# Low parts of the weights in a buffer of their own, with rows 64 bytes off the 512-byte grid

## The reference

```python
h = x + (o * silu(r)) @ gla_w_out          # q, k, v, r, g_low = rms_norm(x) @ gla_w_in
h = h + relu(rms_norm(h) @ mlp_w_up) ** 2 @ mlp_w_down
x = rms_norm(h)
p = rms_norm(x) @ w_in_2                   # q, k, v, three branches, three gates
x = x + (g_a * (attn @ w_attn_o_2) + g_b * (lru @ w_lru_o_2) + g_c * (conv @ w_sc_o_2)) @ w_out_2
x = x + relu(rms_norm(x) @ w_mlp_up_2) ** 2 @ w_mlp_down_2
out = rms_norm(x)
```

## Time and profile before

| | |
|---|---|
| median of 3 runs | 2735.91 us (2735.05 to 2736.26) |
| profiled execution | 2733.07 us, its span 2731.0 us |
| mean granted TensorE clock | 0.996 |
| TensorE busy | 2706.4 us, 99% |
| weight loads busy | 2368.7 us, 87% (beside the matmuls) |
| VectorE busy | 1796.6 us, 66% |
| ScalarE busy | 1348.8 us, 49% |
| DMA | 504 MB, mean 185 GB/s |

### The profile page before, as it was taken

The page is one execution under the profiler, slowest core; times in us unless marked ns, Lnnn a source line. Parts: engine busy times, 40 slices in busy tenths (PEclk is TensorE's granted clock), DMA queues, the critical chain, the costliest instruction groups (busy, mean ns, idle before and its releaser), DMA issues.

```text
span 2731.0 us, 43584 instructions
## 1 busy us (share of the span) xinstructions
PE 2706.4 (99%) x15627; PEld 2368.7 (87%) x15627; DVE 1796.6 (66%) x2074; ACT 1348.8 (49%) x1628; POOL 86.8 (3%) x69
## 2 busy tenths in 40 slices
PE   8999999999999999999999999999999999999998
PEld 7888888888888888888888888888888888888887
DVE  6666867656566567766887666666676566565664
ACT  4546555444444445544575554555554444444443
POOL 3000010000000001200000000000100000000000
PEclk9999999999999999999999999999999999999999
DMA  6564666666566665575546565555656566665653
GB/s 184 161 205 127 185 191 189 191 191 184 192 187 193 189 189 188 181 220 174 173 155 196 188 192 188 190 185 192 191 187 191 185 188 194 187 191 189 189 185 131
DMA packets 507074, 504.45 MB, mean 185 GB/s; under 512 B 17731, under 2 KB 505432, under 8 KB 506984
## 3 DMA queue, kind: packets, MB, share of 16 engines
q1 hardware_dynamic: 505820, 501.60, 59.1%
q10 hardware_dynamic: 1164, 1.63, 0.2%
HBM read 499.50 MB, written 3.67 MB: 184 GB/s over the span
## 4 chain that ended last, share of the span: by engine, by line
PE 98%; DVE 1%; issue 0%; ACT 0%; POOL 0%; DVEq 0%; POOLq 0%; ACTq 0%
PE acc L478 60%; PE acc L480 31%; PE acc L473 3%; PE acc L475 2%; PE misc L578 0%; PE misc L593 0%; PE misc L697 0%; PE misc L535 0%; DVE wsp L1017 0%; PE misc L494 0%; POOL ssq L434 0%; PE misc L560 0%; PE misc L541 0%; PE misc L646 0%; PE misc L595 0%
## 5 line engine op out<-in xcount | busy, mean ns | idle before, releaser
L1017 DVE TENSOR_TENSOR wsp<-raw,wsp 128x1024 fp32r<-128x1024 f32 x944 | 1167.5, 1244 | 597.9 <-ACT wsp L751 567.8
L478 PE MATMUL acc<-xs,wsp 128*128 128x512 f32 x4224 | 1478.9, 395 | 7.8 <-DVE wsp L1017 7.8
L751 ACT ACTIVATE wsp<-raw 128x1024 fp32r<-128x1024 f32 x944 | 992.6, 1056 | 712.2 <-PE acc L480 649.1
L480 PE MATMUL acc<-xs,wsp 128*128 128x256 f32 x4224 | 1180.7, 280 | 0.0
L478 PEld LDWEIGHTS acc<-xs,wsp 128*128 128x128 f32 x4224 | 792.9, 188 | 189.7 <-DVE wsp L1017 9.4
L478 PE MATMUL acc<-hs,wsp 128*128 128x512 f32 x2560 | 890.2, 393 | 0.0
L480 PEld LDWEIGHTS acc<-xs,wsp 128*128 128x128 f32 x4224 | 798.4, 189 | 0.4
L480 PE MATMUL acc<-hs,wsp 128*128 128x256 f32 x2560 | 713.1, 279 | 0.0
L478 PEld LDWEIGHTS acc<-hs,wsp 128*128 128x128 f32 x2560 | 479.5, 187 | 108.7
L480 PEld LDWEIGHTS acc<-hs,wsp 128*128 128x128 f32 x2560 | 482.2, 188 | 0.0
L760 ACT ACTIVATE corr<-acc 128x512 f32<-128x512 f32 x248 | 148.4, 598 | 411.5 <-PE acc L480 392.3
(11 more groups left out here) (213 smaller groups left out, 1016.2 us busy)
## 6 DMA issues: line engine op xcount, KB each, us to landing
raw<-in_w_in SPq DMA_DIRECT2D x224, 512.0 KB, 4.2
raw<-in_mlp_w_up SPq DMA_DIRECT2D x128, 512.0 KB, 4.0
raw<-in_mlp_w_down SPq DMA_DIRECT2D x128, 512.0 KB, 4.1
raw<-in_w_mlp_up SPq DMA_DIRECT2D x128, 512.0 KB, 4.0
raw<-in_w_mlp_down SPq DMA_DIRECT2D x128, 512.0 KB, 4.2
raw<-in_gla_w_in SPq DMA_DIRECT2D x96, 512.0 KB, 3.8
raw<-in_gla_w_out SPq DMA_DIRECT2D x32, 512.0 KB, 4.4
raw<-in_w_out SPq DMA_DIRECT2D x32, 512.0 KB, 4.0
```

The lines of the kernel that those rows point to most:

```text
L478: pe.matmul(acc[:, g, j], wsp[:, slot, t, 0, cols], x[:, k0 + k], start=start, stop=False, skip_group_check=True)
L480: ins = pe.matmul(acc[:, g, j, 1], wsp[:, slot, t, 1, cols], x[:, k0 + k, 0], start=False, stop=stop, skip_group_check=True)
L751: act.activation(wsp[:, slot, :, 0], raw[:, slot], ACT.Copy).then_inc(hi_done, 1)
L1017: dve.tensor_tensor(wsp[:, slot, :, 1], raw[:, slot], wsp[:, slot, :, 0].bitcast(F32), ALU.subtract).then_inc(lo_done, 1)
```

## The change

`wsp` becomes one flat tensor: first the high parts of all slots and row groups, 16 KB, then a gap of 16 elements (64 bytes), then the low parts, 16 KB, and a rest that fills it up to 32 KB + 512 bytes. `w_part(k, slot)` is the high (k = 0) or low (k = 1) part of a slot, four row groups of 256 columns in one run. `both_parts(slot, t)` is one row group with both parts, 16,448 bytes apart. What follows in SBUF moves by 512 bytes. Matmuls, splits, semaphores and their order stay as they are.

```diff
     raw = at("raw", [P, SLOTS, UK, NB])
-    wsp = at("wsp", [P, SLOTS, UK, 2, NB], F32R)
+    LOWS = SLOTS * UK * NB + 16
+    wsp = at("wsp", [P, 2 * SLOTS * UK * NB + P], F32R)
+
+    def w_part(k, slot):
+
+        n = UK * NB
+        return wsp[:, k * LOWS + slot * n:k * LOWS + (slot + 1) * n].rearrange("p (t n) -> p t n", t=UK)
+
+    def both_parts(slot, t):
+
+        row = (slot * UK + t) * NB
+        return wsp[:, 0:2 * LOWS].rearrange("p (k n) -> p k n", k=2)[:, :, row:row + NB]
+
@@ gemm
                         if tokens_out:
-                            pe.matmul(acc[:, g, j], x[:, k0 + k, 0, cols], wsp[:, slot, t], start=start,
+                            pe.matmul(acc[:, g, j], x[:, k0 + k, 0, cols], both_parts(slot, t), start=start,
                                       stop=False, skip_group_check=True)
-                            ins = pe.matmul(acc[:, g, j, 1], x[:, k0 + k, 1, cols], wsp[:, slot, t, 0],
+                            ins = pe.matmul(acc[:, g, j, 1], x[:, k0 + k, 1, cols], w_part(0, slot)[:, t],
                                             start=False, stop=stop, skip_group_check=True)
                         else:
-                            pe.matmul(acc[:, g, j], wsp[:, slot, t, 0, cols], x[:, k0 + k], start=start,
+                            pe.matmul(acc[:, g, j], w_part(0, slot)[:, t, cols], x[:, k0 + k], start=start,
                                       stop=False, skip_group_check=True)
-                            ins = pe.matmul(acc[:, g, j, 1], wsp[:, slot, t, 1, cols], x[:, k0 + k, 0],
+                            ins = pe.matmul(acc[:, g, j, 1], w_part(1, slot)[:, t, cols], x[:, k0 + k, 0],
                                             start=False, stop=stop, skip_group_check=True)
@@ split_hi
-            act.activation(wsp[:, slot, :, 0], raw[:, slot], ACT.Copy).then_inc(hi_done, 1)
+            act.activation(w_part(0, slot), raw[:, slot], ACT.Copy).then_inc(hi_done, 1)
@@ split_lo
-            dve.tensor_tensor(wsp[:, slot, :, 1], raw[:, slot], wsp[:, slot, :, 0].bitcast(F32),
+            dve.tensor_tensor(w_part(1, slot), raw[:, slot], w_part(0, slot).bitcast(F32),
                               ALU.subtract).then_inc(lo_done, 1)
```

## The result

The changed kernel takes 2731.42 us (median of 20 runs, 2730.31 to 2733.04), the kernel before 2737.15 in the 20 runs beside it. The ratio is 0.995, with a 95% interval of 0.9929 to 0.997: a small gain, far from the 4% of the forecast.

What follows compares the result with a forecast made beforehand. TensorE's matmul spacing was taken to bound the kernel. From the profiled 2733.1 us, -98 for low-part loads, -4 for the slower pattern and +2 for waits gave 2633.1; 2.8 more for the median made 2636 us, range 2590 to 2745.

Steps and rivals of the forecast that it cites:

- What the excess is: In the weight stream, each pair of matmuls takes 26.7 ns more than its columns need, 201 us in all.
- The first two readings: In the weight stream: the excess isn't other engines' traffic; a weight load starts with each matmul, reading SBUF beside x.
- The third: The excess is no fixed instruction price: the same instructions also run at 353.8 ns a pair, so two streams stall each other.
- The bound of -13 ns: Long matmul beside the low part's load: its gap falls from 230 to 217 ns, as with the plain fp32 matmuls.
- The term of -98 us: Loads of low parts, 64 bytes off the grid: 7552 pairs gain 13 ns each.
- the slower pattern goes with the change: In the weight stream, 22 of the 236 blocks lose their slower pattern, 0.19 us each: -4 us.
- The +2 us for TensorE's waits: At the hooks of attention and recurrence blocks, a faster TensorE waits more; 7.8 us could double at worst, taken as +2.
- The gv and v blocks: 384 pairs with weights as moving operand, read as two runs: cost 0 to 3 us, taken as 0.
- High parts taken at 0: Loads of high parts beside the short matmul: between 0 and -10 ns a pair, taken as 0.
- No change: Rival, 2736 us, chance 0.29: the full-rate read stalls by itself, or 64 bytes don't affect how the reads collide.
- Slower: Rival, 2785 us, chance 0.16: the long gap settles into the slower pattern, 7.1 ns a pair, +49 us.
- More gained: Rival, 2572 us, chance 0.05: the short gap falls too, a pair takes 326 ns, -160 us with other terms.

Runs made afterwards that it cites:

- the long execution: The kernel before, unchanged, run again until one of its slow executions was profiled: 2761.06 us.

## Why the prediction was wrong

**What bounds the kernel** was right: TensorE's spacing, and no wait near it. The waits for the splits went from 7.8 to 9.6 us and all other work kept its durations.

**What the excess is: the step that failed.** The first two readings hold. The third compared 346.7 with 353.8 ns at equal operands and took it for proof that the whole excess of 26.7 ns is a meeting of two reads, which an offset can end. It proves that for the 6.7 ns between the rhythms only. The runs divide the excess otherwise:

- 7.8 ns are there with a stream that doesn't walk (327.8 ns a pair).
- 18.9 ns need the stream's walk. Against them stand the 6.7 that went with the high parts at 192 bytes and the low parts at 0 (340.0 ns): a part of the excess can indeed be moved by the offset of the loads. If these 6.7 are a part of the 18.9, which no run shows by itself, 12.2 are left that stayed in all nine layouts.
- The offset of the change, low parts at 64 bytes, took nothing from the 346.7 ns. It only ended the 353.3 of the usual blocks.

A load without a walk took nothing away either (346.7), and one with a quarter of the columns 3.4 ns (343.3). So most of the 12.2 ns are probably the stream's own. That isn't shown, as no run has such a stream without a load beside it.

**The bound of -13 ns** rested on the earlier trace rows, where the load was the same and the read half as fast. The prediction read from it that the two reads don't disturb each other there. But the stream that needs new bytes with every column was absent too, and with every column read twice a pair takes 327.5 ns with its loads untouched. So the earlier trace rows can't tell a meeting from a stall of the stream alone, and its 217 ns were no price for an offset. The term of -98 us measured zero: 2886 matmuls beside 2887. The best layout has long gaps of 227 ns and short ones of 113, beside 230 and 117.

**The small terms.** That the slower pattern goes with the change, 22 blocks and -4 us, came true for the usual blocks (3.4 us beside the profiled execution) and is nearly the whole gain of a short execution: about 2736 to 2731 us. Its reason, that the pattern goes together with the excess, was not the right one, since the excess stayed. As a forecast of the median it was undersized, as the profile was of one of the best executions: 36 blocks are slow in another, and in the long ones more than a hundred, where the change gives back some 28 us. The prediction saw three runs within 1.2 us and had no sign of that. The +2 us for TensorE's waits measured +1.8, by luck: they were to come from a faster TensorE, and in its long stretches it wasn't faster. The gv and v blocks were bounded from 0 to 3 us and taken at 0. Beside the profiled execution they cost about 1 us. TensorE alone from 1230 to 1270 us, in the profiled execution of the kernel before, then in the changed kernel:

```profile
1230.00:1270.00 40.00, 40.00 (x232) 1.00 0.65 197
```

```profile
1230.00:1270.00 40.00, 40.00 (x229) 1.00 0.64 195
```

**High parts taken at 0** because neither operand changed its remainder: the number was right, the short gap is still 117 ns. The bound of the whole 10 ns was never reached: with the high parts at 192 bytes the short gap is 113.

**The rivals.** "No change" had the sizes nearly right, 3.3 ns for each matmul and a sixteenth of the stream: the stream without its walk leaves 7.8 ns a pair (5.7 and 2.1), and the walk's 18.9 are a seventeenth of the 320 ns of columns. That this stall comes "whatever is loaded beside it" holds for some 12.2 ns of it at most. Its time was off by the slow rhythm alone. "Slower" was priced for the change and came true for its neighbour: with both parts off by 64 bytes every pair takes 353.3 ns, 2778 us beside the 2785 foretold. "More gained" at 2572 us would have needed the part to go that hangs on the stream's walk: even without the walk the time was 2600.78.

The Trainium skill's two read ports ("TensorE: Matmul & The Clock Gate", step-by-step section) fit the larger part: a load with or without a walk leaves the pair at 346.7 ns. They don't fit the rest. With the same instructions and streams, the place of the loads alone moves a pair from 340.0 to 353.3 ns, and the measurement decides: a load isn't free for the matmul beside it.

**What stays open.** How the 12.2 ns divide between the stream and the mere presence of a load. Why an offset picks its rhythm: the table repeats after 256 bytes in the one case tried, and neither the distance of low to high parts nor that of a load to its stream orders it. Why a stretch falls into one rhythm or the other behind a hook isn't shown either; that it keeps it until the next break is.

## What to carry to other kernels

If a stream of matmuls runs with a constant excess, first read whether it comes in more than one rhythm: the distance between them is a part that can be moved. It is no bound, as 340.0 ns never came in the kernel before. It doesn't explain the rest either, which needs its own test, such as an operand that doesn't walk, before it is priced. A kernel whose times lie in two heaps may have both heaps in its own instruction spacing, so profile one execution of each heap before looking outside. Offsets of operands are cheap to try and not to be foretold: nine layouts of one buffer gave 2683 to 2779 us, and the one that was chosen here was not the best.

## What the runs showed of the hardware

- 18.9 ns of a pair (768 columns of fp32r, granted clock 1.00) hang on a moving operand with new bytes in every column: 346.7 ns with it, 327.8 with one column read again and again, 327.5 with every column read twice. Offsets of the loads alone brought 340.0; if those 6.7 ns are among the 18.9, at most 12.2 are the stream's own.
- Without the walk 5.7 and 2.1 ns are left above the columns: gaps of 219.0 and 108.8 ns for 213.3 and 106.7.
- The offset of the stationary operands, with the moving ones left in place, moves a pair among 340.0, 346.7, 350.0 and 353.3 ns, which are all multiples of 3.33 ns. Low parts at 256 bytes have the rhythms of 0.
- A weight load of 32 columns instead of 128 takes 3.4 ns from most pairs (343.3 beside 346.7) and leaves others at 348.3.
- Behind a pause the stream can fall into either of two rhythms at the same operands, and it keeps it as long as nothing stands between: over 500 us in the long execution (2833 matmuls from 1500 to 2000 us).
